# A two-layer hybrid decoder trunk on one core: first loads taken group by group, a gate applied while the experts' results leave PSUM, the router's shift issued ahead of two weight splits

## The chip, the cores and the metric

One NeuronCore of one Trainium2 chip runs the whole program. The metric is the device time of one execution in microseconds (us), the median of several; lower is better. Five engines work side by side, each in its own program order, and wait for one another through semaphores: PE (TensorE, matrix products into the eight PSUM banks), DVE (VectorE), ACT (ScalarE), POOL (GpSimd) and SP (SyncE, which here only issues DMAs).

## The reference

512 tokens of width 1024, float32, batch 1, two layers. Cut to what the change touches:

```python
c_act = silu(c)
for l in range(2):
    mod = einsum('bd,kde->kbe', c_act, ada_w[l]) + ada_b[l]   # 12 groups of 256 columns per (layer, half)
    sh1, sc1, gt1 = split(mod[0], 3);  sh2, sc2, gt2 = split(mod[1], 3)
    h = rmsnorm(x, norm_mix_g[l]) * (1 + sc1) + sh1
    x = x + gt1 * token_mixer(h, cos, sin, ...)               # attention, delta rule, convolution
    h = rmsnorm(x, norm_ffn_g[l]) * (1 + sc2) + sh2
    # layer 0: dense SwiGLU; layer 1: router (top 2 of 8) and the experts' SwiGLU
    x = x + gt2 * (swiglu(h) if l == 0 else sum_e combine[:, e:e+1] * swiglu_e(h))
return rmsnorm(x, final_norm_g)
```

`cos` and `sin` are of the angles positions * inv_freq. Since `gt2` is one number per feature and `combine` one per token and expert, gt2 * (p0*y0 + p1*y1) is the same as p0*(gt2*y0) + p1*(gt2*y1).

## The kernel before, in words

**Arithmetic.** A float32 product is made of three faster ones: every weight tile and activation is split into a high part (a copy by ACT that rounds) and a low part (a subtraction by DVE), and PE runs high*high, high*low and low*high. `hlo`, `whm` hold high parts of the experts' tiles and `wlm` the low ones (in this stage `hlo` is only a buffer).

**Start.** SP issues the loads in the order of its program: `par` (parameters, 275 KB), `posi` (positions, 256 KB), the modulation weights in groups `ada` g of 1024 KB, `cst` (constants, 1687 KB: identity, ones, masks, the angles' frequencies `invf`), `x` (2048 KB) and the first weight tiles `raw` (512 KB each). The first norm of layer 0 needs groups 0 to 7 (its shift and scale). A group is summed in one of two ways: by DVE, a chain of eight multiply-adds over 256 columns whose result PE then sums over partitions with the constants' ones (`L580`, two short matmuls), or by PE alone, sixteen matmuls of one column (`L573`). Before, PE takes 1, 3, 5, 7 and DVE 0, 2, 4, 6; the groups go through four buffers, so that group g waits for group g - 4. The groups 8 and up come later. Meanwhile ACT squares `x` (`L1177`), PE sums the squares (`L587`), ACT makes the root's reciprocal (`rms`, L1186 and L1187), DVE adds the bias (`modulation`), and `scaled` (DVE) and `shifted` (ACT) make the first h, on which the projections start. POOL computes the rotary angles in 28 dependent steps; ACT needs them for its Sin at 89.16 us.

**Router.** In layer 1 DVE scales h in eight chunks (`scaled(3)`), ACT adds the shift to each (`shifted(3)`, L1197) and PE multiplies by the router's columns (L1037); DVE copies the logits out (L2036) and picks the experts. `high(q)` (ACT, L1229) and `low(q)` (DVE) split pair q of the experts' weight tiles; pairs 0 and 1 are split here, ahead of the experts' loop.

**Experts.** The tokens are sorted into 15 blocks of 128 slots. A block takes 12 pairs of weight tiles; a pair is 12 matmuls of 512 columns. `high` and `low` run three pairs ahead at most: pair q + 3 takes the buffers of pair q. At the end of a block its 128x1024 result lies in PSUM banks 6 and 7, and `results(b)` copies it to `yb`, from which SP stores it to `ys`. In DVE's program block b's items stand in the order of the loop over j = 0..11: `times` before pair j = 3 and 7, `hidden` before 5 and 8, `low`, and `tokens` after pair 9.

**End.** POOL gathers each token's two results from `ys` by indirect DMAs, four chunks of 128 tokens. Per chunk ACT weights the first (`weighted`, L1532), DVE's `combine` adds the weighted second, multiplies by the gate's row `frow[:, 0, :]` and adds the residual; ACT squares it (`root`, L1538), DVE scales (`normed`), PE turns it back, ACT copies it out (`turned_back`, L1545) and SP stores. The gate's row is made by eight PE transposes of broadcast columns (`feature_row`) and one ACT copy (`turned_rows`).

## Time and profile before

| what | value |
|---|---|
| runs, us | 1679.3, 1677.83, 1679.94 (median 1679.3) |
| profiled execution, us | 1681.04, its span 1679.1 |
| PE busy | 1558.0 us, 93% of the span |
| DVE busy | 1182.2 us, 70% |
| ACT busy | 820.3 us, 49% |
| POOL busy | 58.1 us, 3% |
| chain that ended last | PE 86%, DVE 6%, ACT 4%, issue 2%, DMA 1% |
| DMA | 341.37 MB, mean 203 GB/s |

The span is the time from the first to the last instruction of the profiled execution; the execution's own time is 1.9 us longer. The shares of the chain say on which engine the path that ends last lies, whatever else ran beside it.

### The profile page before, as it was taken

The page shows a single profiled execution, that of the slowest core. Times are in us where ns is not written, and L with a number is a line of the kernel's source. Part 1 is how long each engine was busy: PE and PEld are TensorE (multiplying, and loading weights), DVE is VectorE, ACT ScalarE, POOL GpSimd, SP SyncE. Part 2 cuts the span into 40 slices and gives each one's busy share as a digit, 9 for nine tenths or more (in the row PEclk, how much of TensorE's full clock was granted, in tenths as well). Part 3 has the DMA queues.
Part 4 walks back from the last instruction along what each step waited for, and adds up shares of the span by engine and source line. Part 5 has one row for each costly group of instructions (what it writes and reads, how often), then busy time and mean ns, then how long its engine had stood idle before and what let it go on. Part 6 is the DMA issues. An engine that isn't in the chain of part 4 may idle for free.

```text
span 1679.1 us, 22303 instructions
## 1 busy us (share of the span) xinstructions
PE 1558.0 (93%) x8892; PEld 1228.6 (73%) x8892; DVE 1182.2 (70%) x1384; ACT 820.3 (49%) x954; POOL 58.1 (3%) x49
## 2 busy tenths in 40 slices
PE   6999988988999999998999889789999999999993
PEld 4767856766888888885678557478888888888882
DVE  4677885486666665545568854568888888888884
ACT  2354226424222222124542264457777777777765
POOL 6300000000000000000000000020000000000001
PEclk9799988798999999999999888899999999999996
DMA  8352220063555555431111101669999999999964
GB/s 329 101 208 94 89 101 1 33 243 99 177 180 183 182 181 179 143 142 50 64 52 52 51 1 38 221 226 400 391 381 390 391 394 392 382 385 397 392 253 163
DMA packets 93575, 341.37 MB, mean 203 GB/s; under 512 B 9888, under 2 KB 13984, under 8 KB 90784
## 3 DMA queue, kind: packets, MB, share of 16 engines
q1 hardware_dynamic: 91168, 331.56, 54.5%
q0 software_dynamic: 2304, 8.39, 1.4%
q8 instruction: 70, 1.15, 0.3%
q14 instruction: 33, 0.27, 0.0%
HBM read 317.89 MB, written 22.02 MB: 202 GB/s over the span
## 4 chain that ended last, share of the span: by engine, by line
PE 86%; DVE 6%; ACT 4%; issue 2%; DMA 1%; SPq 0%; POOL 0%; DVEq 0%; ACTq 0%; POOLq 0%
PE ps L609 36%; PE ps L1132 10%; PE ps L1130 10%; PE ps L1131 10%; DVE scr L1595 3%; PE ps L573 1%; PE ps L937 1%; PE ps L580 1%; PE ps L911 1%; PE ps L587 1%; DVE scr L1592 1%; PE ps L764 1%; PE ps L756 1%; PE ps L622 1%; DMA cst<-in_consts 1%
## 5 line engine op out<-in xcount | busy, mean ns | idle before, releaser
L609 PE MATMUL ps<-hhi,whi 128*128 128x512 f32 x720 | 299.8, 416 | 2.4 <-ACT sg L1456 2.4
L1592 DVE TENSOR_TENSOR wlm<-rawm,hlo 128x2048 fp32r<-128x2048 f32 x120 | 274.8, 2290 | 36.3 <-ACT hlo L1229 34.6
L1173 ACT ACTIVATE whi<-raw 128x1024 fp32r<-128x1024 f32 (+1 forms) x114 | 125.6, 1104 | 348.3 <-PE ps L609 327.7
L609 PE MATMUL ps<-hhi,wlo 128*128 128x512 f32 x720 | 285.9, 397 | 0.0
L609 PE MATMUL ps<-hlo,whi 128*128 128x512 f32 x720 | 285.0, 396 | 0.0
L1229 ACT ACTIVATE hlo<-rawm 128x2048 fp32r<-128x2048 f32 x120 | 230.0, 1917 | 79.3 <-PE ps L1132 75.4
L1602 DVE TENSOR_TENSOR wlo<-raw,whi 128x1024 fp32r<-128x1024 f32 (+1 forms) x114 | 147.3, 1293 | 151.1 <-ACT whi L1173 149.2
L1131 PE MATMUL ps<-wlm,xgh 128*128 128x512 f32 x480 | 187.7, 391 | 0.0
L609 PEld LDWEIGHTS ps<-hhi,whi 128*128 128x128 f32 x720 | 136.6, 190 | 47.1 <-issue 14.3
L609 PEld LDWEIGHTS ps<-hhi,wlo 128*128 128x128 f32 x720 | 136.4, 189 | 34.4
L609 PEld LDWEIGHTS ps<-hlo,whi 128*128 128x128 f32 x720 | 136.7, 190 | 31.7 <-issue 2.6
L1592 DVE TENSOR_TENSOR wlm<-rawm,whm 128x2048 fp32r<-128x2048 f32 x60 | 137.5, 2292 | 30.7 <-ACT whm L1229 29.9
L1130 PE MATMUL ps<-hlo,xgh 128*128 128x512 f32 x360 | 143.6, 399 | 1.5 <-ACT xgh L1507 1.5
L1132 PE MATMUL ps<-hlo,xgl 128*128 128x512 f32 x360 | 142.8, 397 | 0.0
L1229 ACT ACTIVATE whm<-rawm 128x2048 fp32r<-128x2048 f32 x60 | 114.9, 1916 | 18.2 <-PE ps L1132 18.2
L1131 PEld LDWEIGHTS ps<-wlm,xgh 128*128 128x128 f32 x480 | 90.2, 188 | 21.3
L1595 DVE SCALAR_TENSOR_TENSOR adas<-adah,cact,adas 128x256 f32<-128x256 f32 x196 | 94.9, 484 | 6.6
L1131 PE MATMUL ps<-wlm,hih 128*128 128x512 f32 x240 | 94.0, 392 | 0.0
L1595 DVE SCALAR_TENSOR_TENSOR scr<-scr,par 128x511 f32<-128x511 f32 (+26 forms) x120 | 81.8, 732 | 1.2
L1132 PEld LDWEIGHTS ps<-hlo,xgl 128*128 128x128 f32 x360 | 67.5, 187 | 16.4
L1130 PEld LDWEIGHTS ps<-hlo,xgh 128*128 128x128 f32 x360 | 67.6, 188 | 16.0 <-ACT xgh L1507 1.6
L609 PE MATMUL ps<-ghi,whi 128*128 128x512 f32 x176 | 69.3, 394 | 0.0
(316 smaller groups left out, 2447.3 us busy)
## 6 DMA issues: line engine op xcount, KB each, us to landing
rawm<-in_wm SPq DMA_DIRECT2D x360, 512.0 KB, 7.3
raw<-in_w SPq DMA_DIRECT2D x98, 512.0 KB, 3.6
adah<-in_ada SPq DMA_DIRECT2D x56, 512.0 KB, 4.4
scr<-in_ada SPq DMA_DIRECT2D x20, 1024.0 KB, 6.7
raw<-in_w SPq DMA_DIRECT2D x16, 704.0 KB, 4.1
xs<-scr SPq DMA_DIRECT2D x15, 512.0 KB, 5.4
ys<-yb SPq DMA_DIRECT2D x15, 512.0 KB, 8.8
xg<-xs SPq DMA_DIRECT2D x14, 512.0 KB, 7.0
```

The costliest lines, as they stand in the source:

```text
L573: ins = pe.matmul(ps[:, 7, 2 * g + m:2 * g + m + 1], adar(g)[:, k * 256 + m * P:k * 256 + m * P + P], cact[:, k:k + 1], start=(k == 0), st ...
L580: ins = pe.matmul(ps[:, 7, 2 * g + m:2 * g + m + 1], ada_sum_in(g)[:, m * P:m * P + P], C("ones")[:, 0:1], start=True, stop=True)
L587: ins = pe.matmul(ps[:, 2, :], C("ones"), squares_of(s)[:, k, :], start=(k == 0), stop=(k == DC - 1))
L609: ins = pe.matmul(ps[:, b, :], a, r[:, k0 + k, :], start=(start and first and k == ks[0] and n == 0), stop=(stop and last and k == ks[-1] ...
L1130: pe.matmul(ps[:, bank, :], ah[:, k, :], w_hi, start=(k == 0), stop=False)
L1131: pe.matmul(ps[:, bank, :], ah[:, k, :], w_lo, start=False, stop=False)
L1132: ins = pe.matmul(ps[:, bank, :], al[:, k, :], w_hi, start=False, stop=(k == DC - 1))
L1173: act.activation(whi[:, slot, 0:width], raw[:, slot, 0:width], ACT.Copy).then_inc(sem("hi_ready"), 1)
L1229: act.activation(hi_pair(q), raw_pair(q), ACT.Copy).then_inc(sem("him_ready"), 1)
L1592: return dve.tensor_tensor(out, a, b, op)
L1595: return dve.scalar_tensor_tensor(out=out, in0=a, scalar=s, in1=b, op0=op0, op1=op1)
L1602: dve.tensor_tensor(wlo[:, slot, 0:width], raw[:, slot, 0:width], whi[:, slot, 0:width].bitcast(F32), ALU.subtract).then_inc(sem("lo_ready ...
```

## The change

1. **First loads.** SP now issues `par`, `posi`, the last nine columns of the constants (`invf` and the experts' ranks have been moved there), seven groups of `ada`, the rest of the constants, `x`, the eighth group and then the weight tiles. Groups 0 to 6 have a buffer each; only group 7 waits, for PE's sum of group 0. PE sums groups 0, 2 and 5, DVE 1, 3, 4, 6 and 7, and PE waits for the constants only ahead of the first sum that needs them.
2. **Angles.** POOL waits for positions and the nine columns, not for all constants.
3. **Order in layer 0.** ACT splits the first two weight tiles ahead of `rms(0)`; DVE waits for the root's reciprocal after the two splits and the modulation.
4. **Router.** ACT issues `shifted(3)` ahead of `high(0)` and `high(1)`.
5. **Gate.** The gate's row is made ahead of the experts' loop, in banks 6 and 7. `results(b)` goes from ACT (copy) to DVE (product of PSUM and the gate's row), in DVE's order behind the `low` that is issued at j = 0 of the next block; `combine` loses its product.

```diff
-LANDED_BEFORE = 2 * [2 + (G_FFN - G_IN) // 2] + 2 * [2] + 2 * [G_END - G_FFN] + (RING - 6) * [0]
+BY_PE = (0, 2, 5)
+LANDED_BEFORE = [2 + (G_FFN - G_IN) // 2, 1 + (G_FFN - G_IN) // 2, 1, 1] + 2 * [G_END - G_FFN] + [1, 1, 1] + (RING - 9) * [0]
...
-            at = 5 + 2 * (g % 4) if g < G_IN else 13 + 2 * (g % 2)
+            at = (5, 7, 9, 11, 19, 21, 23, 5)[g] if g < G_IN else 13 + 2 * (g % 2)
...
             sp.dma_start(posi[:], pos.partition_broadcast(P)).then_inc(sem("pos_in"), 16)
-            load_ada(0)
-            load_ada(1)
-            sp.dma_start(cst[:], consts).then_inc(sem("cst_in"), 16)
-            load_ada(2)
-            load_ada(3)
+            sp.dma_start(cst[:, N_CONST - 9:], consts[:, N_CONST - 9:]).then_inc(sem("pos_in"), 16)
+            for g in range(G_IN - 1):
+                load_ada(g)
+            sp.dma_start(cst[:, 0:N_CONST - 9], consts[:, 0:N_CONST - 9]).then_inc(sem("cst_in"), 16)
             sp.dma_start(x[:], xT.rearrange("(c p) s -> p c s", p=P)).then_inc(sem("x_in"), 16)
+            load_ada(G_IN - 1)
             load_tile(0)
             load_tile(1)
-            for g in range(4, G_IN):
-                load_ada(g)
...
-            pool.wait_ge(sem("pos_in"), 16)
+            pool.wait_ge(sem("pos_in"), 32)
             turn(pool.tensor_copy(ang[:, 0, :], posi[:]))
-            pool.wait_ge(sem("cst_in"), 16)
...
                     first_slots()
+                    pe.wait_ge(sem("mod_ready"), 8)
+                    feature_row(mod[:, 88:96], 6)
...
-            rms(0)
             for g in range(2):
                 split(g)
+            rms(0)
...
+                shifted(s)
                 if layer == 1:
                     for q in range(2):
                         high(q)
-                shifted(s)
...
-                            if j == 0 and b:
-                                results(b - 1)
...
-            for g in (0, 2, 4, 6):
+            for g in (1, 3, 4, 6, 7):
                 ada_groups((g,))
-            inverse(0)
             for g in range(2):
                 split(g)
             dve.wait_ge(sem("ada_used"), G_IN)
             modulation(0, 2 * G_IN, 0, 1)
+            inverse(0)
...
+                    def results(b):
+                        dve.wait_ge(sem("tilem_done"), NT * b + NT)
+                        dve.wait_ge(sem("htok_ready"), 5)
+                        if b >= 2:
+                            dve.wait_ge(sem(f"y_out{b % 2}"), 16 * (b // 2))
+                        tt(yb[:, b % 2, :], ps[:, 6:8, :].rearrange("p b n -> p (b n)"), frow[:, 0, :])\
+                            .then_inc(sem("y_ready"), 1)
...
                             low(b * NT // 2 + j + 3)
+                            if j == 0 and b:
+                                results(b - 1)
...
-                        link(tt(y, y, frow[:, 0, :]))
```

PE's first instructions (`L580` is the sum of a group that DVE has made, one record per half of it; `L573` the sum by PE alone, sixteen a group; `L587` the squares of `x`; `L622` the first projection). The first of the `L580` waits for the constants. Before:

```order
L580 MATMUL ps<-cst,scr 128x1 x2
L573 MATMUL ps<-cact,scr 128x1 x16
L580 MATMUL ps<-cst,scr 128x1 x2
L573 MATMUL ps<-cact,scr 128x1 x16
L587 MATMUL ps<-scr,cst 128x512 x8
L573 MATMUL ps<-cact,scr 128x1 x32
L580 MATMUL ps<-cst,scr 128x1 x4
L622 MATMUL ps<-hhi,whi 128x512
```

And of the change, where the same lines are numbered 568, 575, 582 and 617:

```order
L568 MATMUL ps<-cact,scr 128x1 x48
L575 MATMUL ps<-cst,scr 128x1 x4
L582 MATMUL ps<-scr,cst 128x512 x8
L575 MATMUL ps<-cst,scr 128x1 x6
L617 MATMUL ps<-hhi,whi 128x512
```

All of PE's own groups now stand ahead of the squares; behind the squares stand three short sums (groups 4, 6, 7) where two long and two short ones stood.

ACT's instructions at the router of layer 1 (`rstd` the root's reciprocal, `hlo<-rawm` the high parts of pairs 0 and 1, `scr<-scr,mod` the shift, `sq<-ps` the tokens' copy that follows the router's first sums). Before:

```order
L1187 ACT_TABLE_LOAD
L1187 ACTIVATE rstd<-rstd 128x512
L1229 ACTIVATE hlo<-rawm 128x2048 x2
L1197 ACTIVATE scr<-scr,mod 128x512 x8
L1475 ACTIVATE sq<-ps 128x1024 x4
```

And of the change:

```order
L1185 ACT_TABLE_LOAD
L1185 ACTIVATE rstd<-rstd 128x512
L1195 ACTIVATE scr<-scr,mod 128x512 x8
L1227 ACTIVATE hlo<-rawm 128x2048 x2
L1473 ACTIVATE sq<-ps 128x1024 x4
```

The shifts and the two high parts have changed places; DVE's order there is as it was, the two low parts ahead of the logits' copy.

DVE's instructions around the start of the experts' second block (`wlm` low parts, `tm` the product of gate and up, `hil` the low part of the hidden values, `yb` a block's results). Before:

```order
L1592 TENSOR_TENSOR xgl<-ps,xgh 128x1024 [waits xgh_ready]
L1592 TENSOR_TENSOR wlm<-rawm,hlo 128x2048 [waits tilem_done,him_ready]
L1592 TENSOR_TENSOR wlm<-rawm,whm 128x2048 [waits tilem_done,him_ready]
L1592 TENSOR_TENSOR wlm<-rawm,hlo 128x2048 [waits tilem_done,him_ready] x2
L1592 TENSOR_TENSOR wlm<-rawm,whm 128x2048 [waits tilem_done,him_ready]
```

And of the change:

```order
L1580 TENSOR_TENSOR wlm<-rawm,whm 128x2048 [waits tilem_done,him_ready]
L1580 TENSOR_TENSOR wlm<-rawm,hlo 128x2048 [waits tilem_done,him_ready]
L1580 TENSOR_TENSOR yb<-ps,frow 128x1024 [waits htok_ready,tilem_done]
L1580 TENSOR_TENSOR wlm<-rawm,hlo 128x2048 [waits tilem_done,him_ready]
L1580 TENSOR_TENSOR wlm<-rawm,whm 128x2048 [waits tilem_done,him_ready]
```

The result of the block that has just ended now stands between the low parts of the new block's fourth and fifth pair.

## Rows read from the trace of the kernel before

**Rows 1.** Timeline of the first loads' stretch: start, length, engine, line, operation, idle before.
```profile
15.88 1.01 PE L580 MATMUL ps<-cst,scr 128*128 128x1 f32 x4 [15.88 <-DMA cst<-in_consts]
...
16.75 6.96 PE L573 MATMUL ps<-cact,scr 128*128 128x1 f32 x32
...
26.27 4.27 ACT L1177 ACTIVATE scr<-x 128x512 f32<-128x512 f32 x8 [20.87 <-DMA x<-in_xT]
...
31.26 9.91 PE L587 MATMUL ps<-scr,cst 128*128 128x512 f32 x16
...
31.70 5.11 DVE L1595 SCALAR_TENSOR_TENSOR scr<-scr,cact 128x256 f32<-128x256 f32 x7
...
43.20 0.63 ACT L1187 ACTIVATE rstd<-rstd 128x512 f32<-128x512 f32 x1
...
44.88 3.70 DVE L1602 TENSOR_TENSOR wlo<-raw,whi 128x1024 fp32r<-128x1024 f32 x2 [3.32 <-ACT whi L1173]
...
52.03 1.84 PE L580 MATMUL ps<-cst,scr 128*128 128x1 f32 x8
...
54.32 1.78 DVE L1595 SCALAR_TENSOR_TENSOR scr<-x,sclg,rstd 128x512 f32<-128x512 f32 x2
```

**Rows 2.** Busy time by stretch (PE, PEld, DVE, ACT, POOL), clock, DMA share, GB/s.
```profile
0.00:26.20 26.20, 10.32 (x49) 10.32 (x49) 8.60 (x17) 3.12 (x5) 11.42 (x13) 1.00 0.94 351
0.00:33.70 33.70, 17.82 (x75) 16.53 (x76) 10.92 (x20) 8.88 (x15) 18.41 (x19) 1.00 0.96 368
```

**Rows 3.** Timeline of the router's stretch, layer 1.
```profile
1078.20 3.69 ACT L1229 ACTIVATE hlo<-rawm 128x2048 fp32r<-128x2048 f32 x2
1078.33 5.39 DVE L1595 SCALAR_TENSOR_TENSOR scr<-x,sclg,rstd 128x512 f32<-128x512 f32 x8 [5.12 <-ACT rstd L1187]
1081.80 5.00 ACT L1197 ACTIVATE scr<-scr,mod 128x512 f32<-128x512 f32 x8
1082.56 9.82 PE L1037 MATMUL ps<-scr,par 128*8 128x512 f32 x16 [6.50 <-ACT scr L1197]
...
1083.63 4.49 DVE L1592 TENSOR_TENSOR wlm<-rawm,hlo 128x2048 fp32r<-128x2048 f32 x2
...
1092.42 0.68 DVE L2036 COPY yb<-ps 8x512 f32<-8x512 f32 x1 [4.28 <-PE ps L1037]
```

**Rows 4.** Timeline, PE: the experts' first matmul, then the gate's eight transposes.
```profile
1112.52 0.48 PE L1130 MATMUL ps<-hlo,xgh 128*128 128x512 f32 x1 [1.46 <-ACT xgh L1507]
...
1638.00 1.03 PE L1052 MATMUL ps<-cst,mod 128*128 128x128 f32 x8
```

**Rows 5.** Busy time by stretch, as Rows 2: the experts' blocks.
```profile
1116.00:1634.00 518.00, 518.00 (x2362) 422.70 (x2361) 454.18 (x251) 393.35 (x266) 0.01 (x1) 1.00 0.99 379
```

**Rows 6.** Groups of instructions, 1112 to 1636 us: count, busy us, mean ns.
```profile
L1592 DVE TENSOR_TENSOR xgl<-ps,xgh 128x1024 fp32r<-128x1024 f32 x14 | 17.0, 1218 | 0.0
...
L1500 ACT ACTIVATE yb<-ps 128x1024 f32<-128x1024 f32 x14 | 14.1, 1007 | 0.0
```

**Rows 7.** Timeline around the fourth and fifth tile pair of the second block.
```profile
1152.77 2.29 DVE L1592 TENSOR_TENSOR wlm<-rawm,hlo 128x2048 fp32r<-128x2048 f32 x1 [0.49 <-ACT hlo L1229]
1155.96 2.29 DVE L1592 TENSOR_TENSOR wlm<-rawm,hlo 128x2048 fp32r<-128x2048 f32 x1 [0.91 <-ACT hlo L1229]
...
1158.64 0.19 PEld L1130 LDWEIGHTS ps<-hlo,xgh 128*128 128x128 f32 x1
```

**Rows 8.** Timeline of the last combination, DVE and ACT.
```profile
1652.69 1.22 DVE L1592 TENSOR_TENSOR rawm<-rawm,frow 128x1024 f32<-128x1024 f32 x1
...
1655.21 1.06 ACT L1538 ACTIVATE rawm<-rawm 128x1024 f32<-128x1024 f32 x1 [0.45 <-DVE rawm L1592]
...
1663.33 1.14 ACT L1532 ACTIVATE rawm<-rawm,rt 128x1024 f32<-128x1024 f32 x1
...
1669.14 1.06 ACT L1538 ACTIVATE rawm<-rawm 128x1024 f32<-128x1024 f32 x1 [0.67 <-DVE rawm L1592]
...
1674.27 1.02 ACT L1545 ACTIVATE x<-ps 128x1024 f32<-128x1024 f32 x1 [0.68 <-PE ps L1139]
```

More of the change, by code:

```diff
@@ L47 @@
                ("heads", 4 * 8), ("comb_r", 8), ("comb_l", 8), ("col_r", 16), ("col_l", 16), ("col_g", 16),
-               ("sign", 1), ("qscale", 1), ("invf", 1), ("rotm", 1), ("nrotm", 1),
-               ("eps", 1), ("rank", 8), ("before", 128), ("blocks", 16 * 8)):
+               ("sign", 1), ("qscale", 1), ("rotm", 1), ("nrotm", 1),
+               ("eps", 1), ("before", 128), ("blocks", 16 * 8), ("rank", 8), ("invf", 1)):
     C_COLS[_n] = (_at, _at + _w)
@@ L279, in adar, with ada_ring @@
         def adar(g):
-            at = 5 + 2 * (g % 4) if g < G_IN else 13 + 2 * (g % 2)
+            at = (5, 7, 9, 11, 19, 21, 23, 5)[g] if g < G_IN else 13 + 2 * (g % 2)
             return scr[:, at * 1024:(at + 2) * 1024]
+        def ada_ring(g):
+            return (0, 1, 2, 3, 6, 7, 8, 0)[g] if g < G_IN else g % 2
         def ada_landed(engine, g):
             if g < G_IN:
-                engine.wait_ge(sem(f"landed{g % 4}"), 16 * (g // 4) + 16)
+                engine.wait_ge(sem(f"landed{ada_ring(g)}"), 32 if g == 7 else 16)
             else:
-                engine.wait_ge(sem(f"landed{g % 2}"), 16 * (2 + (g - G_IN) // 2) + 16)
+                engine.wait_ge(sem(f"landed{ada_ring(g)}"), 16 * (2 - g % 2 + (g - G_IN) // 2) + 16)
         def squares_of(s):
@@ L368, in by_pe @@
         def by_pe(g):
-            return g < G_IN and g % 2 == 1
+            return g in BY_PE
         def summed(g):
-            return g // 2 + 1 if g < G_IN else g + 1 - G_IN // 2
+            return g + 1 - sum(p < g for p in BY_PE)
         LO_OF = [[6 * layer + at for at in (1, 3, 5, 6)] for layer in range(DEPTH)]
@@ L386, in load_ada @@
                     sp.wait_ge(sem("sincos"), 2)
-                before = g - 4 if g < G_IN else g - 2
-                if 0 <= before < G_IN and g < G_IN:
-                    if by_pe(before):
-                        sp.wait_ge(sem("ada_used"), before + 1)
-                    else:
-                        sp.wait_ge(sem("ada_acc"), summed(before))
-                elif before >= G_IN:
-                    sp.wait_ge(sem("ada_acc"), summed(before))
-                ring = g % 4 if g < G_IN else g % 2
-                sp.dma_start(adar(g), ada[g, :, :]).then_inc(sem(f"landed{ring}"), 16)
+                if g == 7:
+                    sp.wait_ge(sem("ada_used"), 1)
+                elif g >= G_IN + 2:
+                    sp.wait_ge(sem("ada_acc"), summed(g - 2))
+                sp.dma_start(adar(g), ada[g, :, :]).then_inc(sem(f"landed{ada_ring(g)}"), 16)
             def load_ada_half(g, half):
@@ L635, in _ @@
                 if layer == 0:
-                    for g in range(4):
+                    for g in BY_PE:
+                        ada_sum(g)
+                    pe.wait_ge(sem("cst_in"), 16)
+                    for g in (1, 3):
                         ada_sum(g)
@@ L639, in _ @@
                         square_sum(0, k)
-                    for g in (5, 7, 4, 6):
+                    for g in (4, 6, 7):
                         ada_sum(g)
@@ L1494, in gate_half, with turned_rows @@
                         act.activation(sgm[:, half, :], ps[:, 2 * half, :], ACT.Silu).then_inc(sem("sgm_ready"), 1)
-                    def results(b):
-                        act.wait_ge(sem("tilem_done"), NT * b + NT)
-                        if b >= 2:
-                            act.wait_ge(sem(f"y_out{b % 2}"), 16 * (b // 2))
-                        act.activation(yb[:, b % 2, :], ps[:, 6:8, :].rearrange("p b n -> p (b n)"), ACT.Copy)\
-                            .then_inc(sem("y_ready"), 1)
+                    def turned_rows(n, at, out):
+                        act.wait_ge(sem("htok_done"), n)
+                        act.activation(out, ps[:, at:at + 2, :].rearrange("p b n -> p (b n)"), ACT.Copy)\
+                            .then_inc(sem("htok_ready"), 1)
                     act.wait_ge(sem("xt_done"), 1)
@@ L1508, in _ @@
                         .then_inc(sem("xgh_ready"), 1)
+                    turned_rows(5, 6, frow[:, 0, :])
                     act.wait_ge(sem("route_in"), 1)
@@ L1643, in ada_first @@
                 if g >= 4:
-                    dve.wait_ge(sem("ada_used"), g - 3)
+                    dve.wait_ge(sem("ada_used"), {4: 1, 6: 2, 7: 5}.get(g, G_IN))
                 return dve.tensor_scalar(adac[:, g % 4, :], w, cact[:, 0:1], None, ALU.mult)
```

18 lines of the change are left out of this document (5 added, 13 removed).

## The prediction

> **What bounds the kernel now.** I read the page's shares and its chain first: 86% of what ends last is PE, so only stretches in which PE waits can give anything, and work that is put beside PE can only cost. I then went through the timeline for the four places that the diff touches.
>
> *Start.* PE does nothing until the constants land at 15.88, works on groups until x has landed (ACT's squares start at 26.27, released by x), and sums the squares only at 31.26, behind its own group 3. The squares take 9.91 us; behind them come two more groups and four short sums, and DVE's first scaled chunk starts at 54.32 [rows 1]. The reader is to see that the root's reciprocal is done at 43.20 + 0.63 = 43.8 and idle for ten us: the path is PE's, through the groups that stand behind the squares.
>
> *Router.* ACT makes the two high parts from 1078.20 to 1081.9 while DVE's scaled chunks are already there from 1078.33 on; the shifts start at 1081.80 and PE's logits at 1082.56 [rows 3]. The path runs through ACT's shift.
>
> *Experts.* PE is busy for all 518.0 us of the stretch, DVE for 454.2 and ACT for 393.4, at a granted clock of 1.00 [rows 5]. PE is the bound; the rest must stay ahead of it.
>
> *End.* The tail is a pipeline over four chunks in which DVE works almost without a gap, and its last instruction releases the last copy at 1674.27 [rows 8].
>
> **Part 1, the first loads: -6.9 us.** The new order puts x behind seven groups and all constants. In KB of 1024 bytes, before: 275 + 256 + 4 x 1024 + 1687 + 2048 = 8362 KB up to x's end, 8.56 MB. At 26.2 us, when x lands, 26.2 x 351 = 9.20 MB have moved [rows 2], so a load lands when about 0.64 MB more than its place in the order have moved. After: 275 + 256 + 7 x 1024 + 1687 + 2048 = 11434 KB = 11.71 MB, plus 0.64 = 12.35 MB, which the queues have moved at 33.6 us (33.7 x 368 = 12.4 [rows 2]). x lands 7.4 us later than before. The group behind it (g = 7) waits for PE's group 0, which ends long before, so the queues do not run dry.
>
> PE: three groups of its own cost 6.96 us each [rows 1], 21 us. Even if the first started at 12 they would end at 33; the two short sums of groups 1 and 3 take four of the eight records of 1.84 us, 0.9. So PE is free when x is squared. PE's squares start 0.7 us behind ACT's first (0.61 each: 4.27 over 8), at 34.4, and end at 34.4 + 9.9 = 44.3. I keep the 9.9 though it holds two speeds: the sixteen records begin at 0.86 us each, which is 2 x 512 columns at the 1.2 GHz level, and end at 0.43, the 2.4 GHz level, although the granted clock of the window reads 1.00 [rows 1, 2]. All at the low level would be 13.7, all at the high one 6.9. Behind the squares stand six short sums in place of sixty-four long and four short records: 12 records at 1.84/8 = 0.23 each, 2.8 us, to 47.1, and 0.3 for DVE's two small modulation steps: the first scaled chunk at 47.4.
>
> Two other paths must not be later. The root: before it was ready 43.83 - 41.17 = 2.7 us behind the squares (31.26 + 9.91), now at 44.3 + 2.7 = 47.0. DVE: five groups instead of four. The one at 31.70 shows 5.11 for seven of its eight steps, 5.5 in all; group 7 lands at about 12.35 + 1.05 = 13.4 MB, near 36.3 us, and is summed by 41.8; the two splits cost 3.70 and end at 45.5 [rows 1]. Both hold, with 0.4 and 1.9 us to spare. So 54.3 - 47.4 = 6.9. Bounds: -2.8 with the squares all at the low level (34.4 + 13.7 + 3.1 = 51.2, rounded up for a late x), -8.7 where DVE's 45.5 becomes the end.
>
> A rule bears on DVE's part. GpSimd now starts about nine us sooner and so works through all five sums. The Trainium skill, "SBUF — State Buffer", Who interferes with whom, says that a VectorE instruction with two SBUF inputs contends with a GpSimd instruction that reads SBUF. The row at 31.70 was taken with GpSimd at work and its price is already in the 5.5; by the rule every sum costs that, five of them end at 41.8 all the same, since the last starts only when its load lands.
>
> **Part 2, the angles: 0.** They are ready earlier; ACT's Sin is reached at 89 us, and its place moves with the rest of the program. The cover is some 30 us. The nine-column load brings 128 pieces of 36 bytes, which no row of before shows; between nothing and the whole time of the 256 KB positions it changes only when GpSimd starts. I take nothing.
>
> **Part 3, split before root: 0 by itself.** It only makes room for the above: the splits (3.70) stand where DVE waited.
>
> **Part 4, the router: -1.4.** The shifts now follow DVE's chunks: the first at 1079.1, the last ends about 0.7 behind DVE's last chunk (1078.33 + 5.39 = 1083.7), 1084.4. PE's logits start 0.76 behind the first shift, 1079.9, and end at 1089.7, 2.7 earlier. But the high parts, 3.69, now end at 1088.2, and DVE has both low parts (2.25 each) queued ahead of its logits' copy: the second starts at 1088.6 and ends near 1090.9. The copy starts at 1091.0 in place of 1092.42 [rows 3]. What is late next is DVE's low part: of 2.7 gained 1.3 are lost. Bounds 0 and -2.7.
>
> **Part 5, the gate.** *Ahead of the loop: 0.* Eight transposes, 1.03 us, go into a wait of PE of 1.46 [rows 4]; ACT's copy of the row goes into its wait for the first pair. If the transposes ran at half clock (2.1), 0.6 would show.
>
> *In the loop: +0.3.* ACT loses 14 copies of 1.007, DVE gains 14 products. No row shows one from PSUM with the gate's row; the nearest is the 128x1024 difference from PSUM, 1.218 [rows 6]. DVE has (518.0 - 454.2) / 15 = 4.3 us idle in a block [rows 5], so in the mean it fits. Locally it is close: the fourth pair's low part ends at 1152.77 + 2.29 = 1155.06, the product then lasts until 1156.3, and the fifth pair's starts 0.35 later than the 1155.96 of before, ending at 1158.6; PE loads its first weights at 1158.64 [rows 7]. A stall of nothing to 0.1 us in each of 14 blocks; I take 0.3 in all. The Trainium skill, "VectorE: DVE Perf Modes", Specifications, places ScalarE closer to PSUM and VectorE closer to SBUF, which speaks against moving an evacuation to DVE; the rows agree, 1.218 against 1.007, and by either the cost on PE is the slack's, not the 0.2's.
>
> *At the end: -2.8.* The last block's product delays the store by 1.218 - 1.007 = 0.2. DVE loses four products of 1.22 [rows 8]. Chunk 0's square on ACT started at 1655.21, having been idle for 0.45: behind the weighting of chunk 1 it can start only 0.25 earlier, so nearly all of the first product is lost. From there, step by step with the rows' durations: chunk 0's turned copy ends near 1662.3, so the weighting of chunk 3, behind it in ACT's order, starts at 1662.3 in place of 1663.33; DVE combines chunk 3 until 1665.9; ACT squares it at 1666.4 in place of 1669.14; the last copy starts at 1671.4 in place of 1674.27 [rows 8]. Of 4.9 us, 1.0 goes at chunk 0, 0.9 to ACT, 0.2 to the evacuation. Bounds: -1.9 (a gather lands late) and -4.7.
>
> **Sum.** -6.9 - 1.4 + 0.3 - 2.8 = -10.8. It is made against a span of 1679.1 whose execution took 1681.0, 1.7 above the median of the runs; I take the difference off the median, 1679.3: 1668.5.
>
> **Rivals.**
> - *The start gives little.* PE's squares stay at the low level, or x lands some us later than the volumes say: 2.8 in place of 6.9, 1672.6. For it: the long row of one-column matmuls did not bring the high level before, and PE now also waits two us ahead of the squares. Against: the rows at 31.26 rose within the squares. 15%.
> - *Each block stalls.* The product pushes the low parts until PE waits, 0.35 us in each of 14 blocks, 4.9: 1673.1. For it: 0.0 us of slack at the fifth pair. Against: the next pairs have more. 8%.
> - *More than forecast.* Start bound by DVE (-8.7), router -2.7, tail -4: 1664.2. 11%.
> - *Slower.* DVE in the blocks has no slack where it counts and each product is paid in full by PE: 14 x 1.22 = 17.1 in place of 0.3, 1685.3. It decides from (11.1 + 3.4) / 14 = 1.04 us a block on. Against it stand 4.3 idle us a block. 3%.
> - *Nothing comes of it.* Start and end are given back, by a later load or a wait in layer 0: 1678. 3%.
>
> The forecast has the remaining 60%.
>
> **Numbers.** What measurement can tell from no change is about 0.2%, 3.4 us. Faster holds forecast, the first three rivals: 94%. Same 3%, slower 3%. The range takes in the first three rivals to within a little: 1664.0 to 1673.5.
>
> **What would show it.** Right: PE's first instruction near 10 us, x's squares at 33 to 34.5, PE's sum of squares 9 to 11 us long, the first scaled chunk at 47 to 48; the logits' copy right behind the second low part; PE busy all through the blocks; the square of chunk 3 some 11.4 us behind that of chunk 0, where there were 13.9. Wrong: squares' records all at 0.86; gaps of PE released by DVE at the fifth pair of each block; ACT waiting for a gather in the tail.

## The result, and the profile after

The changed kernel took 1669.83 us (median of five, 1667.03 to 1671.84), the kernel before beside it 1679.41 (1677.83 to 1679.94). The ratio is 0.9945, with a 95% interval of 0.9928 to 0.9961: 0.55% faster, 9.6 us. The profiled execution took 1669.83 us, its span 1667.8.

The head of the page, with PE's busy share and its granted clock by slice:

```profile
span 1667.8 us, 22253 instructions
...
PE 1555.6 (93%) x8864; PEld 1226.4 (74%) x8864; DVE 1199.9 (72%) x1403; ACT 809.1 (49%) x939; POOL 60.2 (4%) x49
...
PE   6999987988999999998999889899999999999993
...
PEclk9989988799999999999999888889999999999996
```

Work has moved from ACT (820.3 to 809.1) to DVE (1182.2 to 1199.9), and PE's busy time fell by 2.4 us only (1558.0 to 1555.6): most of what was gained was PE's idle time, which stands in single places, read one by one here.

**Start.** Timeline of the stretch that answers to [rows 1]:

```profile
35.23 4.26 ACT L1175 ACTIVATE scr<-x 128x512 f32<-128x512 f32 x8 [29.73 <-DMA x<-in_xT]
35.91 9.30 PE L582 MATMUL ps<-scr,cst 128*128 128x512 f32 x16 [4.04 <-ACT scr L1175]
38.16 5.85 DVE L1583 SCALAR_TENSOR_TENSOR scr<-scr,cact 128x256 f32<-128x256 f32 x7
...
43.93 3.43 DVE L1590 TENSOR_TENSOR wlo<-raw,whi 128x1024 fp32r<-128x1024 f32 x2
...
45.05 1.40 PE L575 MATMUL ps<-cst,scr 128*128 128x1 f32 x12
...
47.26 0.63 ACT L1185 ACTIVATE rstd<-rstd 128x512 f32<-128x512 f32 x1
47.27 0.16 DVE L1580 TENSOR_TENSOR mod<-ps,par 128x16 f32<-128x16 f32 x1
...
48.00 1.42 DVE L1583 SCALAR_TENSOR_TENSOR scr<-x,sclg,rstd 128x512 f32<-128x512 f32 x2 [0.16 <-ACT rstd L1185]
```

PE now waits for ACT's squares of x, and nothing but the twelve short records of three sums stands behind them. The first scaled chunk is 6.3 us earlier, and what releases it is the root's reciprocal on ACT. DVE had waited for it 0.16 us only: its two splits (the row at 43.93) end at 47.36, and the modulation comes behind them. Behind the chunk the first projection starts at 50.58, where it stood at 57.59.

**Router.** Timeline that answers to [rows 3], with PE's two next steps:

```profile
1071.53 5.39 DVE L1583 SCALAR_TENSOR_TENSOR scr<-x,sclg,rstd 128x512 f32<-128x512 f32 x8 [5.14 <-ACT rstd L1185]
1072.32 5.36 ACT L1195 ACTIVATE scr<-scr,mod 128x512 f32<-128x512 f32 x8 [0.82 <-DVE scr L1583]
...
1079.51 4.49 DVE L1580 TENSOR_TENSOR wlm<-rawm,hlo 128x2048 fp32r<-128x2048 f32 x2 [2.59 <-ACT hlo L1227]
...
1083.94 0.67 DVE L2024 COPY yb<-ps 8x512 f32<-8x512 f32 x1
...
1084.66 1.77 PE L1074 MATMUL ps<-cst,yb 8*128 8x8 f32 x8 [2.13 <-DVE yb L2024]
```

Before, in the same place (here `L1074` is `L1076`):

```profile
1093.15 1.05 PE L1076 MATMUL ps<-cst,yb 8*128 8x8 f32 x8 [0.77 <-DVE yb L2036]
```

The copy stands right behind the second low part. But PE has now waited 2.13 us for it in place of 0.77, and its eight small transposes take 1.77 us in place of 1.05. The windows (PE, PEld, DVE, ACT, POOL, then the granted clock) say why; first of after, then of before, each from PE's transposes on:

```profile
1085.00:1089.00 4.00, 4.00 (x20) 3.98 (x21) 2.16 (x12) 0.64 (x1) 0.00 (x0) 0.50 0.98 365
```

```profile
1092.00:1096.00 4.00, 3.23 (x25) 2.69 (x24) 2.19 (x9) 0.73 (x1) 0.00 (x0) 1.00 0.34 132
```

Behind the wait the granted clock reads 0.50, the level of 1.2 GHz.

**Experts.** The window from the first matmul to the evacuation of the last block, after and before:

```profile
1105.30:1630.70 525.40, 525.39 (x2394) 428.83 (x2395) 469.75 (x272) 383.32 (x254) 2.86 (x3) 1.00 0.98 377
```

```profile
1112.50:1638.40 525.90, 525.88 (x2396) 429.15 (x2397) 456.18 (x258) 393.88 (x267) 2.84 (x3) 1.00 0.98 376
```

PE has no gap in either.

**End.** Timeline that answers to [rows 8]:

```profile
1630.76 1.23 DVE L1580 TENSOR_TENSOR yb<-ps,frow 128x1024 f32<-128x1024 f32 x1 [3.60 <-PE ps L1132]
...
1632.01 0.33 SPq L476 DMA_DIRECT2D ys<-yb  x1
...
1635.39 0.98 POOL L555 DMA_INDIRECT rawm<-ys,slots  x1 [526.56 <-DMA ys<-yb]
...
1646.78 1.04 ACT L1533 ACTIVATE rawm<-rawm 128x1024 f32<-128x1024 f32 x1
...
1657.86 1.05 ACT L1533 ACTIVATE rawm<-rawm 128x1024 f32<-128x1024 f32 x1
...
1662.95 1.02 ACT L1540 ACTIVATE x<-ps 128x1024 f32<-128x1024 f32 x1 [0.68 <-PE ps L1139]
```

The square of chunk 3 stands 11.1 us behind that of chunk 0, where there were 13.9.

**Where the 11.3 us between the two spans went**, cut at four events: the start of the router's first scaled chunk (`scaled(3)` on DVE), the experts' first matmul, the evacuation of the last block, the end.

| stretch | before | after | difference |
|---|---|---|---|
| start to the router's first scaled chunk | 1078.33 | 1071.53 | -6.8 |
| to the experts' first matmul | 34.19 | 33.78 | -0.4 |
| to the last block's evacuation | 525.68 | 525.45 | -0.2 |
| to the end of the span | 40.9 | 37.04 | -3.9 |

### The profile page after: what moved, and what is told of

Its sections match the earlier page's. It is cut to its first block, busy times and chain, and to the rows that moved or that the text cites. A ratio compares the mean times of both kernels' runs of the same rounds, so it can differ in the third digit from the quotient of the medians.

```text
span 1667.8 us, 22253 instructions
## 1 busy us (share of the span) xinstructions
PE 1555.6 (93%) x8864; PEld 1226.4 (74%) x8864; DVE 1199.9 (72%) x1403; ACT 809.1 (49%) x939; POOL 60.2 (4%) x49
## 4 chain that ended last, share of the span: by engine, by line
PE 85%; DVE 6%; ACT 5%; DMA 2%; issue 1%; SPq 0%; POOL 0%; DVEq 0%; POOLq 0%; ACTq 0%
PE ps L604 36%; PE ps L1132 10%; PE ps L1130 10%; PE ps L1131 10%; DVE scr L1583 3%; DMA x<-in_xT 2%; PE ps L935 1%; PE ps L909 1%; DVE scr L1580 1%; PE ps L582 1%; PE ps L762 1%; PE ps L754 1%; PE ps L575 1%; PE ps L617 1%; PE ps L1098 1%
## 5 line engine op out<-in xcount | busy, mean ns | idle before, releaser
L1130 PE MATMUL ps<-hlo,xgh 128*128 128x512 f32 x360 | 143.6, 399 | 0.6 <-issue 0.6
L1130 PEld LDWEIGHTS ps<-hlo,xgh 128*128 128x128 f32 x360 | 67.6, 188 | 15.2 <-ACT xgh L1504 0.8
```

Of the source, the lines that this page charges most:

```text
L1130: pe.matmul(ps[:, bank, :], ah[:, k, :], w_hi, start=(k == 0), stop=False)
```

## The experiments

"Ratio" is that to the kernel before on the same chip, with its 95% interval. "After again" is a further measurement of the kernel after, unchanged. "The scaling" is the start of the router's first scaled chunk.

**a, b and c: the parts alone.** `a_loads` is the kernel before with parts 1 to 3, `c_gate` with part 5, `b_router` with part 4, whose edit is

```diff
+                shifted(s)
                 if layer == 1:
                     for q in range(2):
                         high(q)
-                shifted(s)
```

> The kernel before with the first loads, the angles' wait and the order split before root alone (parts 1 to 3). Theory 1 (the parts add up, as the trace of the change reads: the first projection at 50.6 in place of 57.6, and nothing of it given back later): 7.0 us off, about 1672.4, span 1672.1, PE's first projection at 50.5 to 50.8. Theory 2 (a later stage of layer 0 gives part of it back and router and gate brought the rest): less than 5 us off, and the router's first scaled chunk, at 1078.33 before, less than 5 us earlier.

> The kernel before with ACT's shifts ahead of the two high parts alone (part 4). Theory 1 (the logits' copy comes 1.7 us sooner, but PE goes idle for 2 us ahead of it, behind DVE's low parts, and its next short matmuls run at the lower clock level): the experts' first matmul only 0.3 to 0.6 us earlier than 1112.52, the eight L1076 matmuls 1.7 us long in place of 1.05. Theory 2 (as predicted, the clock does not change): 1.4 to 1.7 us earlier, L1076 1.05. In the median both are within noise.

> The kernel before with the gate in the experts' evacuation alone (part 5). Theory 1 (the loop is PE's and costs nothing, the tail loses three of four products of 1.22): 3.0 to 3.9 us off, about 1675.9; from the last matmul to the last ACT copy 32.2 to 33.1 us in place of 36.1, of it 20.9 from the first weighting on (24.1 before). Theory 2 (the 0.8 us that the last store landed sooner in the trace of the change is chance, not the change's): 33.0 rather than 32.2, with 3.4 to 4.2 us from the store's issue to GpSimd's first gather. Rival (DVE's product stalls PE): the loop longer than 525.7 us from first to last matmul.

Measured: 0.9975 [0.9962, 0.9987] for the loads, 0.9999 [0.9987, 1.001] for the router, 0.9978 [0.9963, 0.9994] for the gate. The three sum to -0.48%, and the whole change gave -0.55%, the same within the intervals; the router's part alone can't be told from nothing. In the traces, the loads bring the first scaled chunk to 47.90 and the first projection to 50.54; the router's copy is early and behind it PE idles 2.12 us, and the experts' first matmul stands 33.8 us behind the scaling, as in after; the gate's loop takes 525.4 us and its tail, from the last matmul's end to the start of the last copy, 32.0 us where before has 36.1. So the gain of the router is lost within the router, not in its meeting with the other parts. One thing more stands in b's trace: its start is that of before, unchanged, and yet its first projection is at 54.43, where before, c and l (below) have 57.29 to 57.73. Its squares took 9.14 us in place of 9.91, and the sixty-four one-column records behind them 8.76 in place of 11.16.

**f and i: what sets x's landing.** In `f_head` all that x's statistics need (ones, eps) goes with the ranks and `invf` into one load of 138 columns ahead of the groups; the rest of the constants goes behind x, group 7 and two weight tiles, and PE waits for it only behind the first projection's matmuls:

```diff
-            sp.dma_start(cst[:, N_CONST - 9:], consts[:, N_CONST - 9:]).then_inc(sem("pos_in"), 16)
+            sp.dma_start(cst[:, N_CONST - 138:], consts[:, N_CONST - 138:]).then_inc(sem("pos_in"), 16)
...
-            sp.dma_start(cst[:, 0:N_CONST - 9], consts[:, 0:N_CONST - 9]).then_inc(sem("cst_in"), 16)
...
             load_tile(0)
             load_tile(1)
+            sp.dma_start(cst[:, 0:N_CONST - 138], consts[:, 0:N_CONST - 138]).then_inc(sem("cst_in"), 16)
```

`i_onecst` is the kernel after with all constants in one load and POOL's angles waiting for it, that is, without part 2.

> The changed kernel with the constants split elsewhere: the first small load takes the last 138 columns (ones, eps, ranks, invf: 552 bytes a partition in place of 36), and the rest of the constants comes behind x, group 7 and two weight tiles; PE waits for that rest only behind the first projection's matmuls. Theory 1 (the start's path is x's landing, then PE's sum of squares): x lands when 1687 KB less have moved, 4 us sooner, at 30.5 to 31.5 us, the first scaled chunk at 44 to 45 in place of 48.0, 3 to 4 us off the changed kernel, about 1666. Theory 2 (DVE, with five sums and two splits, is next in line): the chunk at 45 or later, released by DVE's own splits. Of the small load: if pieces under 512 bytes are what emptied the queues at 4 to 6 us, the first 8 us show over 205 GB/s again (180 in the changed kernel, 211 before); if it is that one more load stands there, 180.

> The changed kernel without part 2: the constants in one load again (in their later place) and GpSimd waiting for it. Theory 1 (the small load of 128 pieces of 36 bytes is what empties the queues at 4 to 6 us, 54 GB/s there where 213 stood before): over 205 GB/s in the first 8 us, x lands 0.8 to 1.0 us sooner than 35.2, and the first scaled chunk comes 0.8 to 1.0 sooner than 48.0; GpSimd starts near 29 and ends near 70, ahead of ACT's Sin at 82, so nothing else is lost: 0 to 1 us faster than the changed kernel. Theory 2 (the small load costs nothing, the dip is the queues' own start): 180, x at 35.2. Rival: the angles now late, ACT waits at its Sin.

Measured for f: 1665.78 us, ratio 0.9929 [0.991, 0.9947], 4.0 us below after's median; by the two ratios it is 2.7. Timeline of `f_head`:

```profile
30.62 4.27 ACT L1177 ACTIVATE scr<-x 128x512 f32<-128x512 f32 x8 [25.05 <-DMA x<-in_xT]
31.31 9.85 PE L582 MATMUL ps<-scr,cst 128*128 128x512 f32 x16
...
43.20 0.63 ACT L1187 ACTIVATE rstd<-rstd 128x512 f32<-128x512 f32 x1
...
43.94 1.48 DVE L1585 SCALAR_TENSOR_TENSOR scr<-x,sclg,rstd 128x512 f32<-128x512 f32 x2 [0.41 <-ACT rstd L1187]
```

What stands behind x moves with it, but less at each step: x 4.6 us, the first scaled chunk 4.1, the first projection (at 47.23) 3.4. For i: 1670.03 us, ratio 0.9948 [0.9929, 0.9968], as after. x lands at 33.86, 1.4 us sooner, and the scaled chunk stands at 47.20, 0.8 sooner, but the first projection at 50.54 is no better than after's 50.58. What was gained went on DVE: its 8-column `sclg` took 1.05 us and the first scaled chunks 1.85, in after 0.37 and 1.42; why is open. POOL ends at 72.5 in place of 50.8, and ACT's Sin at 83.97 does not wait for it: part 2 is worth nothing, as forecast. The windows of 4 to 6 us in after, which has the nine-column load, in `i_onecst`, which has none, and in `g_all` (below), which has the load of 138 columns (last column GB/s):

```profile
4.00:5.00 1.00, 0.00 (x0) 0.00 (x0) 0.00 (x0) 1.00 (x1) 0.00 (x0) 1.00 0.52 31
5.00:6.00 1.00, 0.00 (x0) 0.00 (x0) 0.22 (x1) 0.49 (x3) 0.00 (x0) 1.00 0.35 78
```

```profile
4.00:5.00 1.00, 0.00 (x0) 0.00 (x0) 0.00 (x0) 1.00 (x1) 0.00 (x0) 1.00 0.97 170
5.00:6.00 1.00, 0.00 (x0) 0.00 (x0) 0.23 (x1) 0.58 (x3) 0.00 (x0) 1.00 0.74 266
```

```profile
4.00:5.00 1.00, 0.00 (x0) 0.00 (x0) 0.00 (x0) 1.00 (x1) 0.00 (x0) 1.00 0.42 53
5.00:6.00 1.00, 0.00 (x0) 0.00 (x0) 0.23 (x1) 0.54 (x3) 0.00 (x0) 1.00 0.46 128
```

In these two us 81 of after's 109 packets are under 512 bytes, and 9 of i's 84. The hole's size varies. Over the first 8 us after moved 180 GB/s and the six further profiles with its loads 178 to 207, with x landing between 33.97 and 35.31; without a small load i moved 220 and the four profiles with before's loads 200 to 237. Against i's one profile the nine-column load costs x between 0.1 and 1.4 us, and after's own profile is one of the late ones. Whether the narrow pieces make the hole or one more load in the row is not shown: with pieces of 552 bytes f has a small one (127 and 247, 209 over the 8 us) and g a deep one (53 and 128, 194).

**j: the router and the clock.** Two matmuls that nobody reads are added behind the router's logits:

```diff
+                    for k in range(2):
+                        pe.matmul(ps[0:NE, 1, :], PR("rw", k * NE, NE), h[:, k, :], start=True, stop=True)
```

> The changed kernel with two more 512-column matmuls behind PE's logits, into a free bank and read by nobody (1.7 us), so that PE does not go idle while DVE makes the low parts. Theory 1 (PE's idle time ahead of L1074 is why its next matmuls run at the lower level): L1074's successor 1.05 us long in place of 1.77, the first sixteen token matmuls 1.97 in place of 3.67, the slots' cast 0.7 to 1.0 us sooner against the logits' copy (12.4 in the changed kernel, 11.5 before). Theory 2 (chance of the clock): still near 1.77.

Measured: 1670.43, ratio 0.9954 [0.9932, 0.9977]. Timeline and then windows of `j_warm`:

```profile
1082.20 1.05 PE L1076 MATMUL ps<-cst,yb 8*128 8x8 f32 x8 [0.42 <-DVE yb L2026]
1083.19 1.97 PE L1045 MATMUL ps<-cst,scr 128*128 128x128 f32 x16
```

```profile
1082.00:1085.00 3.00, 2.80 (x24) 2.69 (x24) 1.61 (x9) 0.69 (x1) 0.00 (x0) 1.00 0.98 360
...
1093.00:1102.00 9.00, 8.96 (x68) 8.72 (x66) 3.07 (x3) 1.49 (x3) 6.92 (x5) 0.83 0.49 190
```

With PE kept at work until 0.42 us before its transposes, these and the token matmuls behind them take 1.05 and 1.97 us again, and the slots are ready 11.1 us behind the copy in place of 12.4. So the wait lowered the clock. The other profiles agree: in all six with a wait of 2.11 to 2.15 us there the transposes take 1.75 to 1.81, in all eight with 0.42 to 0.77 they take 1.05. But the experts' first matmul stands 33.6 us behind the scaling against 33.8: the clock falls later, in the tokens' turns, where it reads 0.83 and after's read 1.00 (1096.5 to 1105.5 us). Between these two profiles the filler has moved the loss, not removed it; why the clock fell there is open.

**d and k: the low parts out of the router's path.** In `d_lowlate` DVE makes no low part before the logits' copy:

```diff
                 scaled(s)
-                if layer == 1:
-                    low(0)
-                    low(1)
...
-                    low(2)
+                    low(0)
+                    low(1)
```

and `low(2)` follows the tokens' low part. `k_slots` is that, with block 1's tokens fetched at tile 20 of block 0 and not at tile 16.

> The changed kernel with DVE's low parts of the experts' pairs 0 and 1 behind the slots' calculation (and that of pair 2 behind the tokens' low part) in place of ahead of the logits' copy. Theory 1 (DVE's low parts are what made the logits' copy late, and the idle time of PE that they made is what lowered its clock): copy right behind PE's logits, 1.3 us sooner, idle time of PE ahead of L1074 under 1 us, L1074 back at 1.05 us; the experts' first matmul 2.0 to 2.4 us earlier against the first scaled chunk of the router (33.8 us behind it in the changed kernel, 34.2 before, 31.5 here); 2 us off the changed kernel. Theory 2 (the clock falls there for another reason): 1.3 us, L1074 still 1.7. Rival: the low parts are now late for the first experts' pairs and nothing is gained.

> d_lowlate with SP's load of the second block's tokens four tiles later in the first block (t = 20 in place of 16). In d_lowlate the experts' first matmul came 29.5 us behind the router's first scaled chunk in place of 33.8, but PE stood still for 4 us at pair 8, since SP waited for GpSimd's scatters ahead of the loads of tiles 16 and on. Theory 1 (that wait is all that took the gain back): no stall at pair 8, at most 0.5 us at pair 10, from the first scaled chunk to the last experts' matmul 555 to 556.5 us (560.6 in d_lowlate, 559.2 changed, 559.9 before), 3 us off the changed kernel. Theory 2 (the scatters themselves, slower beside DVE's low parts, then hold block 1): the stall moves to the second block's tokens at t = 20, and 560 remains.

Measured: d 1669.1, ratio 0.9946 [0.9927, 0.9965]; k 1666.57, 0.9932 [0.9915, 0.995]. In both the experts' first matmul stands 29.5 us behind the scaling where after has 33.8, two more than I had expected. Of these 4.2 us, 1.4 are the copy, which now stands right behind PE's logits, and 2.9 lie between the copy and the tokens' turns (`L1067`), 9.65 us in place of 12.53: the granted clock never falls. The window from the transposes into the turns in d:

```profile
1080.00:1097.00 17.00, 13.33 (x115) 12.87 (x116) 12.67 (x43) 6.60 (x7) 4.64 (x3) 1.00 0.15 26
```

After reads 0.50 and 0.57 in its windows 1085 to 1089 and 1089 to 1096. And the length of a wait alone does not decide it: before `L1082` (`L1080` in d and k) PE waits 2.08 us in before, j, d, k and g alike, and behind this wait the clock reads 0.68 in before and 0.72 in j, but 1.00 in d, k and g.

In d the gain is given back within the experts' first block, seen in its timeline:

```profile
1112.99 0.33 SPq L471 DMA_DIRECT2D xg<-xs  x1
1113.36 14.89 SPq L464 DMA_DIRECT2D rawm<-in_wm  x16
1120.42 1.91 ACT L1227 ACTIVATE whm<-rawm 128x2048 fp32r<-128x2048 f32 x1 [4.24 <-issue]
1124.78 0.19 PEld L1130 LDWEIGHTS ps<-whm,hih 128*128 128x128 f32 x1 [4.15 <-issue]
```

SP waits for GpSimd's scatters before it can fetch block 1's tokens (`xg`), and the weight tiles are queued behind that. The scatters end later against the loop, since the loop starts earlier, and four of them are slower, beside DVE's low parts: 2.41, 1.65, 2.08 and 2.47 us. In after two are above the usual 0.95, with 1.22 and 2.36. In k the gap there is gone, and one remains when those tokens are needed (`PEld L1130` at 1131.69, 2.95 us behind `hil`). From the scaling to the last matmul's end d takes 560.6 us, after 559.2, k 558.4, where I had expected 555 to 556.5. Theory 1 is right on the slots' path, but the gain comes back within the experts' first block, in d more than all of it and in k all but 0.8 us, mostly as the wait for block 1's tokens. Of the 2 to 3 us by which k is faster than after, by the ratios and by the medians, the traces place less than one in the edit.

**h: is there slack in the loop?** The gate's product is done a second time in every block but the last, into a row that nobody reads:

```diff
+                        if b < NB - 1:
+                            link(tt(frow[:, 1, :], ps[:, 6:8, :].rearrange("p b n -> p (b n)"), frow[:, 0, :]))
```

**g and after again** stood beside it: `g_all` is after with the edits of f and k together, `after_2` is after unchanged.

> The kernel after with the gate's product from PSUM done twice in each block but the last: the second one's result is read by nobody, and it stands on DVE right behind the first, ahead of the fifth pair's low part. It prices the cover of the loop. Theory 1 (DVE has no slack at the fifth pair, so a further product shows in full on PE): 14 x 1.1 us = 15 us, with gaps of PE released by DVE at the fifth pair of each block, 1685 us. Theory 2 (the pairs behind it have slack enough, and the slack at the fifth pair is larger than the 0.0 us that I read, since PE reached its weights late for another reason): nothing to 0.5 us a block, 1670 to 1676 us.

> The kernel after with two edits that were tried apart: the constants split so that all that x's statistics need comes in one load of 138 columns ahead of the groups (f_head), and the low parts behind the slots' calculation with block 1's slots loaded at pair 20 (k_slots). If the two act on different stretches, they add: against the kernel before, f_head alone gave a ratio of 0.9929 and k_slots 0.9932 where the kernel after gave 0.9945, so the product is 0.9929 x 0.9932 / 0.9945 = 0.9916, about 1664 us against 1678. In its trace the first scaled chunk stands near 44, and the experts' first matmul 29.5 us behind chunk 3's scaling. The rival: what either gave is the chip's scatter, and together they read 0.993, as each alone.

> The kernel after unchanged, on the same chip as the two beside it, so that their differences to it are read in one place. Expected: 0.9945 of the kernel before within its interval; the store of the last block's row lands 2.6 us behind its issue again, and PE's transposes of the logits take 1.77 and 3.67 us behind 2.1 us of idle. If these two are an accident of one profile, they read 3.4 us, or 1.05 and 1.97.

Measured: h 1680.69 us, ratio 1.0002 [0.9989, 1.0015]; g 1664.43, 0.9898 [0.9876, 0.9919]; after again 1669.91, 0.9932 [0.9906, 0.9958]. Waits of PE's two queues in `h_twice`, 1120 to 1630 us (line waited for: us in total, times, longest):

```profile
PEld ps L1130 <- DVE wlm L1580: 15.5, 14, 1.1
```

```profile
PE ps L1130 <- DVE wlm L1580: 9.6, 14, 0.7
```

Its loop takes 538.2 us from first to last matmul, after's 525.0: 13.2 us, or 0.94 for each of the 14 products. Each is 1.1 us of DVE, so the slack at the fifth pair was near 0.2 us, and theory 1 is right but for this slack. Neither row of waits gives the price: the weight load's 1.11 is too much, since it was to start ahead of need, and the matmul's 0.68 too little, since its start is 1.07 us behind the one before it where 0.23 is the pace, and the next follows in 0.34. 0.84 + 0.11 = 0.95 is what the loop shows. (The whole kernel is 10.8 us slower than after again by the medians, less than the loop's 13.2: outside the loop h's profile is some 2 us shorter than that of after again, in code that is the same.) PE in the second block of `h_twice`:

```profile
1150.68 0.39 PE L1132 MATMUL ps<-hlo,xgl 128*128 128x512 f32 x1
1151.75 0.50 PE L1130 MATMUL ps<-hlo,xgh 128*128 128x512 f32 x1 [0.68 <-DVE wlm L1580]
1152.09 0.39 PE L1131 MATMUL ps<-wlm,xgh 128*128 128x512 f32 x1
```

And DVE in the second block of after:

```profile
1147.70 1.22 DVE L1580 TENSOR_TENSOR yb<-ps,frow 128x1024 f32<-128x1024 f32 x1
1148.83 2.28 DVE L1580 TENSOR_TENSOR wlm<-rawm,hlo 128x2048 fp32r<-128x2048 f32 x1
```

The product holds DVE for 1.13 us, not 1.22: the next instruction starts before its end.

g is the fastest kernel here, 5.5 us below after on the same chip. By the two ratios it is 0.9898 / 0.9932 = 0.9966 of after, where the product of the two edits' own ratios had 0.9971. That fits two gains that add, but the intervals are as wide as either gain, and the traces show mainly one: g's first scaled chunk stands at 44.44, 3.1 us ahead of that of after again, and from the scaling to the last matmul's end it takes 558.5 us where after again takes 559.2. After again repeats both of the readings that it was run for: the transposes took 1.80 us behind a wait of 2.14, and the first gather starts 3.37 us behind the store's issue.

**l: why the last store lands sooner.** In after, c, d, f, g, h, i, j, k and after again GpSimd's first gather starts 3.36 to 3.38 us behind the store's issue; in before, a and b, in which ACT evacuates, 4.17, 4.02 and 3.98. `l_shift` is the kernel before with

```diff
                             high(q + 3)
+                            if b == 10 and j < 8:
+                                act.activation(small[:, 204 + j:205 + j], C("ones")[:, 0:1], ACT.Copy)
```

> The kernel before with eight further ACT instructions of one column, unread, one behind each of the first eight pairs of block 10, where ACT idles. It is about the store of the last block's row, which lands 3.4 us behind its issue in the three kernels in which ACT evacuates the row and 2.6 us in the nine in which DVE does. In the three an instruction load of 0.01 MB on queue 14 falls into the store, and the last packets go out singly; in the nine there is none there. Theory 1 (that load, not the writing engine, makes it late; its place follows the count of instructions ahead of it on ACT): eight more instructions put the load earlier, before ACT's last splits or out of the store, and the store lands in 2.6 us though ACT writes the row. Theory 2 (the writing engine makes it late): 3.4 us as before, wherever the load stands. A third outcome, that the load stays in the store, would mean that it is not ACT's and would leave it open. The median moves by less than a measurement tells: a ratio of 0.999 to 1.001.

Measured: ratio 0.9993 [0.9979, 1.0006]. The DMA rates in the four us from the store's issue on, in steps of 0.1 us, before and then `l_shift`:

```profile
GB/s 0 0 0 0 0 0 0 0 369 492 369 328 369 451 369 369 328 532 410 328 410 0 41 41 0 41 41 0 41 0 0 0 0 0 0 0 0 0 0 0
...
q14 instruction: 1, 0.01, 1.2%
...
ys<-yb SPq DMA_DIRECT2D x1, 512.0 KB, 3.4
```

```profile
GB/s 0 0 0 0 0 0 0 0 410 451 328 410 369 492 410 369 451 451 328 410 369 1 0 0 0 0 0 0 0 0 0 0 0 0 0 0 0 0 0 0
...
ys<-yb SPq DMA_DIRECT2D x1, 512.0 KB, 2.6
```

Queue 14 (`q14`) brings instructions. With its load some nine us earlier, at 1630.5 where before has it at 1640.0, the store lands in 2.6 us though ACT writes the row, and the gather starts 3.37 us behind its issue. Theory 1 holds. The steps of 41 GB/s at the end of before's store are single packets of 4 KB; that they are the share of one DMA engine which the instruction load had held up is a reading, not shown.

## Why the prediction was right

Forecast 1668.5, measured 1669.8, in the range; the likeliest case is the one that came. The sum of -10.8 stands against -11.3 between the two profiled spans. That it is so close is in part luck: the router gave 1.0 us less than its term, the tail 1.1 more and the loop 0.5 more. It was taken off the runs' median, though the profiled execution of before was 1.7 us above that: the two executions differ by 11.2, the medians by 9.6. Off the execution's own 1681.0 the same sum gives 1670.2. Which of the two is the better base no single profile tells; the stretch from the first projection to the router alone reads 1018 to 1026 us in the profiles here with its code unchanged.

- **Start, -6.9.** -6.3 at the first scaled chunk, -7.0 at the first projection, -6.8 at the router. x landed at 35.2 and not 33.6: the step "a load lands when about 0.64 MB more than its place in the order have moved" holds, but the queues had moved 361 GB/s by 34 us where I counted with 368, and the nine-column load, whose price I took as nothing, is part of it: without it (i) they moved 370 and x lands at 33.86. The 9.9 of the squares measured 9.3. What stands behind them came out in another order than I had it. The short sums, my path, took 1.40 and not 2.8: 0.12 us a record, with the granted clock at 1.00, where those of [rows 1] took 0.23 with it at 0.50. (After's eight short records ahead of the squares took 0.23 each too, 1.87 us, where I had counted four; nothing hung on them.) The path ended on the root's reciprocal, which I had 0.4 us inside; its time behind the squares is 2.7 us as read. And DVE, to which I had given 1.9 us to spare, had 0.16: group 7 was summed by 44.0 in place of 41.8, since it landed later and its sum took 6.2 us in place of 5.5, and the splits ended at 47.4 in place of 45.5. In a, h, i, j, k and after again DVE does not wait for the root at all: there its own work is what ends last.
- **What of the start was luck.** Between the first scaled chunk and the first projection after takes 2.6 us and before 3.3; no step of mine has these 0.7, and kernels with after's order at the start show either value (i, k and h 3.3, a, d, j and after again 2.6). And the start that I read in before is the usual one, but not the only one: against b's first projection, at 54.43 with the same code, the loads would have gained 3.9 us.
- **Angles and splits, 0.** Right (i).
- **Router, -1.4.** The step "the copy starts at 1091.0 in place of 1092.42" is right: the copy is 12.4 us behind the scaling where it was 14.1. What failed is that the gain went on from there. PE's wait grew by 1.4 us, its clock fell, and of 1.7 us only 0.4 arrived. b shows it without the other parts, and j that the wait lowers the clock. How much of the loss is the clock's own, no run isolates: in j the clock falls later and the gain is lost all the same, and in d and k, where it stays at 1.00 and the gain arrives, the low parts stand elsewhere too.
- **Gate in the loop, +0.3.** -0.2 measured, and no gap of PE. The slack was as read: I had 0.04 us left at the fifth pair and h shows near 0.2, the difference being in part the 0.1 by which each DVE instruction overlaps the next. h pays what the rivals feared, 0.94 us a block, and ends level with before; so some 0.2 us a block is all that stands between the kernel and that loss.
- **Tail, -2.8.** -3.9. The steps of chunk 0 and chunk 3 stand as worked out (11.1 us between the squares, 11.4 forecast), and from the first weighting to the last copy it takes 20.9 in place of 24.1, -3.2. The remaining 0.6 is the store: the evacuation is 0.2 longer, as forecast, and the landing 0.8 sooner, since the instruction load that had fallen into it is elsewhere (l). It stood in the trace of before, as one row of the DMA view, and the prediction left it out.

## What to carry to other kernels

Where a step on a neighbouring engine comes earlier, PE may wait longer for the next one: here a wait of PE that grew from 0.8 to 2.1 us was followed by some ten us at a granted clock near half. The gain of such a step is to be followed until the clock is back, and a filler at one place may only move the loss. Slack that is read as the time between a producer's end and PE's next weight load is right to some 0.2 us: before a second instruction is put there, double the first one. Loads at the start are worth ordering by volume: f moved 1.7 MB from ahead of x to behind it, x landed 4.6 us sooner and the first projection stood 3.4 us earlier. But the other paths to the same point have to be added up with the same care, for DVE's was within 0.2 us of becoming the end.

## What the runs showed of the hardware

- With a load of 128 pieces of 36 bytes, 4.5 KB in all, among the first loads, after's queues moved 31 and 78 GB/s in the two us from 4 to 6, against 166 and 260 in before and 170 and 266 in i. The depth differs from profile to profile, and with pieces of 552 bytes both a small hole (f, 127 and 247) and a deep one (g, 53 and 128) were seen.
- A load of 0.01 MB of instructions that meets a 512 KB store made it land in 3.4 us in place of 2.6, and eight instructions of one column elsewhere on ACT moved it away.
- The same 8 transposes took 1.77 us behind 2.13 us of idle and 1.05 behind 0.77, at granted clocks of 0.50 and 1.00. Behind another wait, of 2.08 us in five profiles, the clock read 0.68, 0.72 and three times 1.00.
- Consecutive DVE instructions overlap by 0.1 us: in after a product of 128x1024 whose record is 1.22 us long holds DVE for 1.13.
- GpSimd's scatter took 0.95 us alone and 1.65 to 2.47 beside DVE's low parts, whose two inputs lie in SBUF. In three of d's four slow ones, and in after's of 2.36, it ends 0.82 to 0.84 us behind the end of the low part. The Trainium skill, "SBUF — State Buffer", Who interferes with whom, says that a VectorE instruction with two SBUF inputs contends with a GpSimd instruction that reads SBUF. The trace agrees, if the scatter, which takes its places from the `slots` tile, counts as such a read; no run isolates it.
